# A mixture-of-experts stage regrouped: every block takes 32 rows of each of two experts, and a block's down projection runs behind the next block's gate/up

## What is computed

```python
def _hier_moe(h, w_coarse, b_coarse, w_fine, b_fine, w_gate, w_up, w_down):
    t = h.reshape(n * t_len, d)
    coarse_logits = (t @ w_coarse) + b_coarse          # 4 groups
    grp = argmax(coarse_logits)
    fine_sel = fine_logits_of(grp)                     # 8 experts of the chosen group
    top_v, top_i = lax.top_k(fine_sel, 2)
    p_exp = softmax(top_v) * p_grp
    for e in range(32):
        hid = silu(t @ w_gate[e]) * (t @ w_up[e])      # 1024 -> 256
        out = out + combine[:, e:e+1] * (hid @ w_down[e])   # 256 -> 1024
```

## Time and profile before

| | |
|---|---|
| median of 3 runs | 526.67 us (526.08 to 532.02) |
| profiled execution, its own time | 528.73 us |
| its span, from first to last instruction | 527.0 us |
| granted clock, mean | 0.98 |
| first gate/up, first silu, last silu | 273.0, 277.0, 491.6 us |
| PE busy | 478.6 us, 91% |
| bytes moved by DMA | 146.01 MB, mean 277 GB/s |

### The profile page before, as it was taken

The page is one execution under the profiler, slowest core; times in us unless marked ns, Lnnn a source line. Parts: engine busy times, 40 slices in busy tenths (PEclk is TensorE's granted clock), DMA queues, the critical chain, the costliest instruction groups (busy, mean ns, idle before and its releaser), DMA issues.

```text
span 527.0 us, 8895 instructions
## 1 busy us (share of the span) xinstructions
PE 478.6 (91%) x3289; PEld 283.4 (54%) x3290; DVE 237.0 (45%) x513; ACT 102.1 (19%) x209; POOL 183.0 (35%) x282
## 2 busy tenths in 40 slices
PE   6999999999999999999679999989979998979784
PEld 3887777777777645555434444444434444434331
DVE  4219999999993520335742222112212221122146
ACT  5130011011112523323511111111101111110213
POOL 3010915665575800101153434443433433442100
PEclk9989999999999999999789999999999999999998
DMA  8995005200000299936769999999999999999887
GB/s 328 319 391 157 0 2 206 113 2 0 1 1 1 87 363 424 393 146 205 308 227 420 416 410 390 418 418 419 415 387 419 422 418 419 395 414 420 268 280 260
DMA packets 43992, 146.01 MB, mean 277 GB/s; under 512 B 10240, under 2 KB 18448, under 8 KB 32697
## 3 DMA queue, kind: packets, MB, share of 16 engines
q1 hardware_dynamic: 37242, 131.06, 64.7%
q0 software_dynamic: 4960, 9.45, 4.8%
q10 hardware_dynamic: 1759, 5.06, 2.5%
HBM read 136.83 MB, written 15.53 MB: 289 GB/s over the span
## 4 chain that ended last, share of the span: by engine, by line
PE 77%; DMA 7%; issue 6%; DVE 4%; ACT 3%; SPq 1%; POOL 1%; DVEq 0%; POOLq 0%; ACTq 0%
PE bank L1374 27%; PE bank L1577 10%; PE bank L1457 10%; PE bank L1597 9%; PE bank L1572 9%; PE bank L1367 4%; DMA region_x<-in_w_up 2%; DMA region_w<-y_rows 2%; PE bank L1587 2%; PE bank L1483 2%; DVE region_m L1256 1%; DVE region_m L1258 1%; ACT region_m L722 1%; PE bank L1523 1%; DMA y_rows<-region_m,slast 1%
## 5 line engine op out<-in xcount | busy, mean ns | idle before, releaser
L1374 PE MATMUL bank<-region_m,region_w 128*128 128x256 f32 (+1 forms) x576 | 142.3, 409 | 0.0
L1374 PEld LDWEIGHTS bank<-region_m,region_w 128*128 128x128 f32 x576 | 110.3, 192 | 30.4 <-issue 0.6
L1256 DVE TENSOR_TENSOR region_m<-region_m,bank 128x128 f32<-128x128 f32 x30 | 8.7, 288 | 160.5 <-ACT region_m L722 160.5
L1457 PE MATMUL bank<-region_w,z 128*128 128x512 f32 x128 | 56.7, 595 | 0.2 <-ACT z L647 0.2
L1015 DVE SCALAR_TENSOR_TENSOR z<-region_m,z 128x512 f32<-128x512 f32 x60 | 48.7, 812 | 0.0
L1015 DVE SCALAR_TENSOR_TENSOR region_x<-region_m,region_x 128x512 f32<-128x512 f32 x56 | 45.9, 820 | 0.0
L1597 PE MATMUL bank<-region_w,region_m 128*32 128x512 f32 x272 | 40.3, 598 | 2.8 <-DVE region_m L1258 2.8
L807 POOL TENSOR_TENSOR region_m<-region_x 128x512 f32<-128x512 f32 x4 | 20.2, 5053 | 63.6 <-ACT region_m L601 32.4
L1457 PEld LDWEIGHTS bank<-region_w,z 128*128 128x128 f32 x128 | 23.8, 190 | 28.0 <-issue 26.3
L878 POOL COPY gcol<-gidx 128x1 uint32 (+1 forms) x30 | 5.4, 181 | 95.1 <-DVE region_m L1245 95.1
L589 ACT ACTIVATE region_x<-bank 128x256 f32<-128x256 f32 (+1 forms) x40 | 14.2, 407 | 123.6 <-PE bank L1374 104.0
(11 more groups left out here) (240 smaller groups left out, 642.8 us busy)
## 6 DMA issues: line engine op xcount, KB each, us to landing
region_w<-in_w_down SPq DMA_DIRECT2D x16, 1024.0 KB
region_w<-in_w_gate SPq DMA_DIRECT2D x12, 1024.0 KB, 16.1
region_w<-in_w_up SPq DMA_DIRECT2D x12, 1024.0 KB
region_m<-in_w_down SPq DMA_DIRECT2D x12, 1024.0 KB
region_w<-in_w_in SPq DMA_DIRECT2D x4, 2048.0 KB, 18.7
region_m<-in_w_gate SPq DMA_DIRECT2D x8, 1024.0 KB
region_m<-in_w_up SPq DMA_DIRECT2D x8, 1024.0 KB
slot<-in_w_gate SPq DMA_DIRECT2D x4, 1024.0 KB
```

Source lines behind the costliest of these rows:

```text
L1374: ins = mm(ps[2 * bank + j][:, 0:LEN[j]], sec[name][:, k, c * P:(c + 1) * P], hT[:, k, CUT[j]], start=(k == 0), stop=(k == KC - 1))
L1457: ins = mm(ps[2 * (t % 2) + j][0:n, :], z[:, k, t * P:t * P + n], w_out_sb[:, k, j * 512:(j + 1) * 512], start=(k == order[0]), stop=(k == ...
```

## The change

- **Blocks.** Every block holds up to 32 rows (HT) of each of a pair's two experts. Pair m has as many blocks as the larger of its two experts has 32-row shares, at least one.
- **Order and pairing.** `turns()` sorts experts 8 to 31 downward by their counts in tiles 0 to 2 (three times the largest eight), and neighbours in that order form pairs. Experts 0 to 7 keep their places. It runs behind `place(2)`, now at tile 4; `rank(2)` moves up within the last output tile on PE; the rows of tiles 0 to 2 are placed together by GpSimd afterwards.
- **PE.** gate/up(g), transpose of hid(g-1), four token transposes for g+1, down(g-1). The one-column matmul goes. gate/up also waits for `s_hid`. In round 0 there is a body for a pair's first pair and loops for the others; in later rounds one loop per pair, with the waits for the weights and two `If`s inside, that pick the slots of the previous pair's or of this pair's down.
- **ACT, DVE.** silu(g+1) stands ahead of y_out(g), the hidden copy of g-1 ahead of the product of g.
- **SP.** In all rounds a pair is reloaded together: both gates and ups once gate/up of the pair's last block is done, then both downs once its last down is done.

```diff
-NBLK = NPAIR + NE + (2 * NTOK - NE * (T // 2 + 1)) // T
+HT = T // 2
+NBLK = (2 * NTOK + NPAIR * HT - 1) // HT
...
             with sp.Fori(1, NE // NSLOT) as it:
-                for i in range(NSLOT - 2):
-                    reload(i, *turn(it, i), range(3))
-                ends_of = [(i, *turn(it, i)) for i in range(NSLOT - 2, NSLOT)]
-                for which in (range(2), range(2, 3)):
-                    for i, e, last in ends_of:
-                        reload(i, e, last, which)
+                for i in range(0, NSLOT, 2):
+                    last = sp.value_load(bound[0:1, bass.ds(it * (NSLOT // 2) + (i // 2 + 1 - NSLOT // 2), 1)],
+                                         min_val=1, max_val=NBLK)
+                    pair = [(i + k, turn(it, i + k)) for k in range(2)]
+                    for which in (range(2), range(2, 3)):
+                        for j, e in pair:
+                            reload(j, e, last, which)
...
+            silu(0, 0)
+            silu(0, 1)
+            y_out(0, 0)
+            silu(1, 0)
+            y_out(0, 1)
+            silu(1, 1)
+            y_out(1, 0)
+            with act.Fori(1, pairs - 1) as q:
+                silu(q + 1, 0)
+                y_out(q, 1)
+                silu(q + 1, 1)
+                y_out(q + 1, 0)
...
+            def keys():
+                dve.wait_ge(s_rank, NT - 2)
+                link(nc.vector.scalar_tensor_tensor(out=key, in0=early[:, NSLOT:NE], scalar=float(NE), in1=iota32[:, NSLOT:NE],
+                                                    op0=ALU.mult, op1=ALU.add))
             def turns():
+                for r in range(0, NE - NSLOT, 8):
+                    link(nc.vector.max(top[:, r:r + 8], key))
+                    if r < NE - NSLOT - 8:
+                        link(nc.vector.scalar_tensor_tensor(out=key, in0=key, scalar=top[:, r + 7:r + 8], in1=key,
+                                                            op0=ALU.is_lt, op1=ALU.mult))
+                link(nc.vector.tensor_copy(topi, top))
+                link(nc.vector.tensor_scalar(topi, topi, NE - 1, None, ALU.bitwise_and))
+                link(nc.vector.tensor_copy(expert_at[:, NSLOT:NE], topi))
+                marks(0, NT - 2, s_again)
+                link(pairs_of(0, NT - 2))
+                placed(0, NT - 2).then_inc(s_place, NT - 2)
                 nc.vector.tensor_copy(bound[0:1, ORDER:ORDER + NE], expert_at[0:1, :])
...
             for t in range(NT):
                 n = TROWS[t]
+                if t == NT - 1:
+                    keys()
                 if t >= 2:
                     place(t - 2)
-                if t == 3:
+                if t == NT - 1:
                     turns()
...
+            nc.vector.tensor_tensor(of_pair[:, 1:NPAIR + 1], nbi2[:, :, 0], nbi2[:, :, 1], ALU.max)
...
+            def block_of(q, b):
+                if not isinstance(q, int) or b:
+                    turned(q * 2 + b)
+                hidden(q, b)
+                tokens_out(q * 2 + (b + 2))
+                move(q + 1, b)
...
-                        if k == KC - 1:
+                        if k == KC // 2 - 1:
                             rank(t - 2)
...
+                if isinstance(first, int):
+                    weights()
+                    gate_up(first, i)
+                    next_tokens(1)
+                    with pe.If(end > first + 1):
+                        with pe.Fori(first + 1, end) as g:
+                            gate_up(g, i)
+                            turn_hidden(g - 1)
+                            next_tokens(g + 1)
+                            down(g - 1, i, it)
+                    return
+                with pe.Fori(first, end) as g:
+                    weights()
+                    gate_up(g, i)
+                    turn_hidden(g - 1)
+                    next_tokens(g + 1)
+                    with pe.If(g < first + 1):
+                        down(g - 1, (i - 2) % NSLOT, it if i else it - 1)
+                    with pe.If(g > first):
+                        down(g - 1, i, it)
...
+            blocks = end_of(bound[0:1, NPAIR:NPAIR + 1])
+            turn_hidden(blocks - 1)
+            down(blocks - 1, NSLOT - 2, NE // NSLOT - 1)
```

More of the change, by code:

```diff
@@ L1093, in turns @@
                 nc.vector.tensor_copy(bound[0:1, ORDER:ORDER + NE], expert_at[0:1, :])
-                for t in range(2):
-                    marks(t, s_again)
-                pairs_of(0, 2)
             def select(t):
@@ L1263, in _ @@
             move(0, 1)
-            with nc.vector.Fori(0, pairs) as q:
+            for b in range(2):
+                block_of(0, b)
+            with nc.vector.Fori(1, pairs) as q:
                 for b in range(2):
                     block_of(q, b)
-                    tokens_out(q * 2 + (b + 2))
-                    move(q + 1, b)
+            turned(pairs * 2)
             with nc.vector.If(odd > 0):
-                block_of(pairs, 0)
+                hidden(pairs, 0)
+                turned(pairs * 2 + 1)
             dve.wait_ge(s_w12, 1)
@@ L1607, in pair @@
-            def pair(it, i, first, after, end):
-                for part in range(2):
-                    pe.wait_ge(s_wexp[i][part], it * 16 + 16)
-                with pe.If(after > first + 1):
-                    with pe.Fori(first, after - 1) as g:
-                        block_of(g, (i, i), it)
-                for part in range(2):
-                    pe.wait_ge(s_wexp[i + 1][part], it * 16 + 16)
-                block_of(after - 1, (i, i + 1), it)
-                with pe.If(end > after):
-                    with pe.Fori(after, end) as g:
-                        block_of(g, (i + 1, i + 1), it)
@@ L1620, in pair_of, with pair, weights @@
-            def pair_of(it, i, first=None):
-                if first is None:
-                    first = pe.value_load(bound[0:1, bass.ds(it * NSLOT + i, 1)], min_val=0, max_val=NBLK - 1)
-                after, end = bounds(bound[0:1, bass.ds(it * (NSLOT // 2) + (i // 2 + ENDS), 1)])
-                pair(it, i, first, after, end)
-                return end
+            def pair(it, i, first, end):
+                def weights():
+                    for part in range(2):
+                        for half in range(2):
+                            pe.wait_ge(s_wexp[i + half][part], it * 16 + 16)
+                if isinstance(first, int):
[18 more added lines that the diff above has]
+                        down(g - 1, i, it)
@@ L1628, in _, with end_of @@
             keep_busy(10)
             pe.wait_ge(s_tab, 1)
-            round0 = [bounds(bound[0:1, ENDS + m:ENDS + m + 1]) for m in range(NSLOT // 2)]
+            def end_of(at):
+                return pe.value_load(at, min_val=1, max_val=NBLK)
+            round0 = [end_of(bound[0:1, m + 1:m + 2]) for m in range(NSLOT // 2)]
             pe.wait_ge(s_mv, 1)
             tokens(0, KC // 2).then_inc(s_xt_ps, 1)
-            end = 0
-            for m, (after, last) in enumerate(round0):
-                pair(0, 2 * m, end, after, last)
-                end = last
+            first = 0
@@ L1638, in _ @@
+            for m, end in enumerate(round0):
+                pair(0, 2 * m, first, end)
+                first = end
             with pe.Fori(1, NE // NSLOT) as it:
[L1639 removed]
+                first = end_of(bound[0:1, bass.ds(it * (NSLOT // 2), 1)])
                 for i in range(0, NSLOT, 2):
[L1641 removed]
+                    end = end_of(bound[0:1, bass.ds(it * (NSLOT // 2) + (i // 2 + 1), 1)])
+                    pair(it, i, first, end)
+                    first = end
```

188 lines of the change are left out of this document (80 added, 108 removed).

## The result

| | before | after |
|---|---|---|
| median | 528.17 us, same chip | **544.67 us** (543.88 to 547.72, 4 runs) |
| ratio | 1 | **1.031** [1.024, 1.039] |
| profiled execution, own time; span | 528.73; 527.0 us | 544.53; 542.7 us |
| granted clock, mean | 0.98 | 0.949 |
| PE busy | 478.6 us, 91% | 489.3 us, 90% |

Slower by 3.1%; forecast were 547.0 us and "slower" with 0.90. The page first: 40 slices of 13.6 us each.

What follows compares the result with a forecast made beforehand. Expert stage with two nearly equal limits, TensorE and weight DMA. Last silu 510 + 35.4 + 2.3 = 547.7 us span; own time 549.4, less 2.06 gives 547.3 us (+3.9%). Range 541 to 553, wider 538 to 561.

Steps and rivals of the forecast that it cites:

- The period: TensorE's time per expert block: from about 7.0 to 6.5 us, bounds 5.8 to 7.7.
- The 0.2 set aside for the two branches: In each expert block: 6.5 us taken where the working summed to 6.3, with two new branches and four more waits.
- Rival B: Each expert block pays for its branches through late code: period 7.1 to 7.7, 557 to 568 us, chance 0.20.
- Mixed blocks cost nothing, 32 blocks, rounds of 13 10 5 4: Expert stage: a two-expert block takes TensorE 3.81 us against 3.85; 32 blocks instead of 30, rounds 13, 10, 5, 4.
- Routing: Sorting moved to tile 4, hidden behind that tile's product by 0.9 us: cost 0, bounds -1 and +3.5 us.
- within 1 us of 273: Sign for the routing: the first gate/up was to begin within 1 us of 273 us.
- The empty queue: Weight reloads in rounds 0 and 1: some 30 us in which the queue has nothing to move.
- 5 + 5 + 16 + 5: The empty queue's gaps in us, as pairs 5 to 8 wait for blocks 4, 7, 12 and 15.
- the 2.0 us set aside for an inner hole: TensorE idle inside a block, counted with 1.2 for the round start in placing block 15 at 376.6 us.
- The last silu: End of the expert stage: at 509 to 510 us, taken as 510 against 491.6 before, set by the last weights.
- some 9 us: TensorE's wait for weights before each of blocks 29, 30 and 31; the sign said 7 to 12 us.
- The tail: After the last silu: 35.4 us as before, plus 2.3 for a down ahead of the last transpose.

Runs made afterwards that it cites:

- e7: Kernel before with its own blocks, pairs, routing and reload, but gate/up(g) put ahead of down(g-1): 563.22 us, ratio 1.066.
- e3: Changed kernel with experts 0 to 7 paired, so round 0 has 10 blocks instead of 13: 527.71 us, ratio 0.998.
- e6: Changed kernel with its regrouping, but the order of before inside a block on all engines: 557.46 us, ratio 1.055.
- e1: Changed kernel with sorted experts 12 to 23 put ahead of 0 to 11: 543.01 us, ratio 1.029.
- e2: Changed kernel with the sorted pairs of rounds 1 to 3 reversed, fewest rows first: 554.27 us, ratio 1.051.
- e12: e3 with the order of before inside a block: 535.01 us, ratio 1.017 against the kernel before.
- e11: e7 with only the first quarter of each weight part of rounds 1 to 3 loaded, outputs wrong: 550.15 us, ratio 1.046.
- e10: e7 with a shorter TensorE program, one loop per pair in which branches pick gate/up and down: 578.28 us, ratio 1.098.

## Why the prediction was right

- **The period.** Forecast 6.5 by a working that gave 6.3; measured 6.20. Transpose to down is 0.72 us, down to the next gate/up 1.74, gate/up 3.81, as in the working. The 0.2 set aside for the two branches was not needed where a loop turns within a pair, but where a pair is a single block the period is 6.3 to 6.5 (blocks 25 to 27), and a round's first blocks have 0.9 and 1.2 us more (at 357.8 and 421.5 us). Rival B's period did not come. Its mechanism may be real all the same, as the long holes of e7 suggest. "Runtime: NRT & Kernel Launch" of the Trainium skill (Instruction fetch mechanics) describes a stall at a taken branch to a page not held; e7's holes of 4.8 to 11.5 us stand where the program branches, between a down and the next gate/up, and fit it, while the hole inside its gate/up has no branch and is not what that sentence describes.
- **Mixed blocks cost nothing, 32 blocks, rounds of 13 10 5 4.** As forecast: 3.81 us each, 32 silus.
- **Routing.** Taken as 0, and the first silu is at 277.31 against 277.02. But that is luck, as two errors cancelled: the first gate/up began at 271.1 us, 1.9 earlier and outside the "within 1 us of 273", and took 2.1 us longer at the half clock, which the prediction did not have.
- **The empty queue.** The "5 + 5 + 16 + 5" was right in kind and in where its gaps lie: forecast from 297, 317, 338 and 372 us, measured at 299 to 302, 320 to 323, 338 to 353 and 371 to 374. It was too large in size. The share from 281 to 377 us is 0.85 against 1.02 when full, which makes some 16 us of an empty queue instead of 31. Block 12 was forecast at 353.9 and came at 350.7, block 15 at 376.6 and came at 370.5; the 2.0 us set aside for an inner hole did not come. e3 closes the largest gap and takes back 17 us.
- **The last silu.** Forecast 509 to 510, measured 509.56. Here too terms cancelled. The working starts at block 15, which came 6.1 us earlier than forecast. From there to the end of the last wait at 503.65 us the queue moved 404 GB/s, not 417, its gap at 371 to 374 included; the same bytes thus took some 4 us more. And the last gate/up took 5.84 us at the half clock instead of 3.81 (2.0 us). What is left over is under 1 us. That the sum came out within 1 us is luck. "DMA: Bandwidth & Descriptors" of the Trainium skill (Where 436 GB/s comes from) gives 358 GB/s for the HBM side and a ceiling of 435. The trace decides against the first, as every full stretch shown here passes 358; none of them passes 435.

```profile
370.50:503.65 133.15, 103.66 (x1296) 50.85 (x1296) 23.86 (x64) 13.98 (x32) 44.96 (x94) 0.89 1.01 404
```

- **Waits before blocks 29, 30, 31 of "some 9 us".** Four waits, 5.9 to 7.8 us, before 28 to 31, 28 us in all: the forecast's 27 in four pieces, one of them under the 7 that it gave as the least.
- **The tail.** Forecast 37.7 us, measured 542.7 - 509.56 = 33.1. Most of the added 2.3 is there: the last output copy starts 5.41 us behind the last silu (3.36 before), 2.05 more. But the last scatter takes only 2.3 us until the y rows are asked for (5.3 before, beside the x rows' loads), and the chain's wait for y rows is 9.5 us instead of 11.0. The tail was thus over-sized by 4.6 us, more than the 2.6 between 547.3 and 544.7; the rest of it is offset by the median of after, which lies 0.1 above its profiled execution where before's 526.67 lay 2.06 under.

```profile
514.97 0.60 ACT L728 ACTIVATE region_m<-bank 128x512 f32<-128x512 f32 x1 [2.16 <-PE bank L1615]
...
516.35 0.99 POOL L913 DMA_INDIRECT y_rows<-region_m,slast  x1 [0.51 <-issue]
...
518.64 0.32 SPq L541 DMA_DIRECT2D region_w<-y_rows  x1
```

- **What only the runs showed.** The prediction had the mechanism, and its working lets a longer period end later (its B) as e6 does: 522.5 us for the last silu at a period of 7.0. The two errors came afterwards, in the expectations. e1's took it that the order of the pairs in rounds 1 to 3 matters, e2's that it costs nothing; swapping the halves brings 1.7 us, and putting the large pairs last costs 10. e12's held PE's period for worthless once round 0 has ten blocks; a shorter one keeps the queue fuller (7 to 10 us).

## What to carry to other kernels

Where a slot is refilled only when its last reader is done, count not the blocks but the time until each slot comes free: moving blocks into the round ahead of the first refill empties the queue, and its bytes are waited for at the end. A faster engine in front of a transfer that binds is worth what it brings forward in requests: here 12.8 us with 13 blocks in round 0, 7 to 10 with ten. And branches that cost little in a small loop came with tens of microseconds of standstill when more variants of a body were laid beside each other: look for idle "issue", above all inside an unbroken run of matmuls, and at the packets of instruction loads near it.

## What the runs showed of the hardware

- Code is fetched in 16 KB pieces. Every standstill of TensorE over 4 us without a releaser has one to three of them in it or just ahead of it (five in e7, three in e11, up to 11.5 and 9.5 us), but most pieces come while it works (20 of 32 in e7), so a piece has no fixed price: 0.3 us on average in after, 1.0 in e11, 2.0 in e10.
- TensorE's granted clock was down at the half level (1.2 GHz) behind the 3.0 us of idle before the first tokens and behind each of the last four waits of the kernel after, and the next gate/up took 5.5 to 6.4 us instead of 3.8; behind the 2.4 us of idle at the same place in before it stayed at the full level (2.4 GHz). Where a wait for weights ends the stage, this adds 2.0 us to it.
- SP itself stood for 18.1 us in issuing one up-weight load of the kernel after, at 454.4 us, with the queue full (before: 20.1 us at 433.8); whatever stands behind it in SP's program is asked for that much later.

```profile
454.44 18.13 SPq L438
```
